# The causal mask of stick-breaking attention, moved from VectorE into the score matmuls

## What is computed

```python
def stick_breaking_attention(q, k, v):
    scale = 1.0 / math.sqrt(q.shape[-1])
    def block(args):
        qb, i = args
        z = jnp.einsum('bhqd,bhkd->bhqk', qb, k) * scale
        q_idx = i * Q_BLOCK + jnp.arange(Q_BLOCK)
        strict = key_idx[None, :] < q_idx[:, None]
        log_one_minus = jnp.where(strict, jax.nn.log_sigmoid(-z), 0.0)
        suffix = lax.cumsum(log_one_minus, axis=3, reverse=True) - log_one_minus
        w = jnp.where(strict, jnp.exp(jax.nn.log_sigmoid(z) + suffix), 0.0)
        return jnp.einsum('bhqk,bhkd->bhqd', w, v)
```

## Time and profile before

| | |
|---|---|
| runs | 2357.04, 2357.75 (median), 2361.81 us |
| profiled execution | 2354.45 us |
| its span, first to last instruction | 2352.7 us |
| mean granted clock of PE, share of full speed | 0.975 |
| PE busy | 2206.1 us, 94% |
| DVE busy | 1676.1 us, 71% |
| ACT busy | 908.8 us, 39% |
| the stick stage | 1963.2 to 2092 us of the span |
| the soft stage | 2092 to 2205 us |

### The profile page before, as it was taken

The page is one execution under the profiler, slowest core; times in us unless marked ns, Lnnn a source line. Parts: engine busy times, 40 slices in busy tenths (PEclk is TensorE's granted clock), DMA queues, the critical chain, the costliest instruction groups (busy, mean ns, idle before and its releaser), DMA issues. The chain is left out here.

```text
span 2352.7 us, 31764 instructions
## 1 busy us (share of the span) xinstructions
PE 2206.1 (94%) x12629; PEld 1967.4 (84%) x12629; DVE 1676.1 (71%) x2797; ACT 908.8 (39%) x1193; POOL 619.2 (26%) x354
## 2 busy tenths in 40 slices
PE   5999989988999998999999899999999898989997
PEld 2888777876799998999999899999999676667775
DVE  6555677873489999889876787778787646566543
ACT  4222234333233333566653233333333433456423
POOL 0000042322347667333334433333331000000000
PEclk8999999999999999999999999999999899999999
DMA  7667410012237777899999999999996222111222
GB/s 259 207 228 235 158 50 1 1 72 72 90 115 248 248 242 241 316 353 338 358 353 374 373 359 352 353 359 350 357 350 238 79 84 66 51 45 55 81 90 72
DMA packets 177524, 486.59 MB, mean 207 GB/s; under 512 B 13632, under 2 KB 80320, under 8 KB 165856
## 3 DMA queue, kind: packets, MB, share of 16 engines
q1 hardware_dynamic: 140512, 350.33, 43.6%
q0 software_dynamic: 36864, 134.23, 14.8%
HBM read 429.98 MB, written 52.43 MB: 205 GB/s over the span
## 5 line engine op out<-in xcount | busy, mean ns | idle before, releaser
L1087 PE MATMUL ps<-h_high,u_high 128*128 128x384 f32 (+1 forms) x1216 | 428.4, 352 | 22.1 <-POOL u_low L1305 12.4
L1089 PE MATMUL ps<-h_high,u_low 128*128 128x384 f32 (+1 forms) x1216 | 420.3, 346 | 0.0
L1088 PE MATMUL ps<-h_low,u_high 128*128 128x384 f32 (+1 forms) x1216 | 420.1, 345 | 0.0
L1087 PE MATMUL ps<-w_high,v_high 128*128 128x384 f32 x1024 | 343.8, 336 | 7.2 <-DVE w_low L1722 7.2
L1089 PE MATMUL ps<-w_high,v_low 128*128 128x384 f32 x1024 | 342.9, 335 | 0.0
L1088 PE MATMUL ps<-w_low,v_high 128*128 128x384 f32 x1024 | 342.9, 335 | 0.0
L1087 PEld LDWEIGHTS ps<-h_high,u_high 128*128 128x128 f32 x1216 | 230.5, 190 | 36.6 <-POOL u_low L1305 14.6
L1455 ACT ACTIVATE v_high<-v_raw 128x2048 fp32r<-128x2048 f32 x64 | 122.6, 1916 | 347.9 <-PE ps L1089 338.5
L1087 PE MATMUL ps<-h_high,w_high 128*128 128x512 f32 x560 | 227.5, 406 | 16.9 <-DVE w_low L346 4.8
L1089 PEld LDWEIGHTS ps<-h_high,u_low 128*128 128x128 f32 x1216 | 230.2, 189 | 8.0
L1088 PEld LDWEIGHTS ps<-h_low,u_high 128*128 128x128 f32 x1216 | 230.9, 190 | 7.0
(11 more groups left out here) (436 smaller groups left out, 4182.9 us busy)
## 6 DMA issues: line engine op xcount, KB each, us to landing
v_raw<-in_peer_v SPq DMA_DIRECT2D x64, 1024.0 KB, 6.7
w_raw<-in_w SPq DMA_DIRECT2D x95, 512.0 KB, 3.5
u_first<-in_uT SPq DMA_DIRECT2D x32, 1024.0 KB, 6.1
u_second<-in_uT SPq DMA_DIRECT2D x32, 1024.0 KB, 6.2
xT<-in_late_w SPq DMA_DIRECT2D x56, 512.0 KB, 4.5
gelu_up<-gelu SPq DMA_DIRECT2D x128, 192.0 KB, 6.8
gates<-gates_sb SPq DMA_DIRECT2D x12, 2048.0 KB, 12.2
weighted<-gelu_up SPq DMA_DIRECT2D x64, 384.0 KB, 6.8
```

Source lines behind the costliest of these rows:

```text
L1087: pe.matmul(out, wh, mh, start=start, stop=False)
L1088: pe.matmul(out, wh, ml, start=False, stop=False)
L1089: return pe.matmul(out, wl, mh, start=False, stop=stop)
```

## The change

The 32 stick masks leave DVE. For a stick item PE follows the score matmul with a second one, identity times `cmask[:, 0]`, that accumulates into the last 128 columns of the same bank; `scored` is counted up by this one. ACT's `exps` of a stick item waits for `scored` and no more for `masked`, which from now on counts soft items alone. DVE's two masks ahead of slot 0 go, and in slots 0 to 14 the masks behind each `finish`; the first mask left is that of item 32, in slot 15. Two waits are new: PE waits once for the causal masks (`made`), and ACT before item 0 for DVE's last scaling of `k.xT` (`rt1_copied` at 2), since `rest[:, 0]` is written by that item's sigmoid.

```diff
--- before.py
+++ after.py
@@ -2068,6 +2068,7 @@
                 kind, h, i = items[2 * p]
                 if p == 0:
                     pe.wait_ge(act_read, read_by(BY_ACT, PROJECTED))
+                    pe.wait_ge(made, 3)
                 if p == HALF:
                     pe.wait_ge(act_read, read_by(BY_ACT, soft_ready))
                     pe.wait_ge(dve_read, read_by(BY_DVE, soft_ready))
@@ -2080,8 +2081,11 @@
                         q, key = sq[a, h // 2], sk[a, h // 2]
                     else:
                         q, key = mq[0:QKD, h + s], mk[0:QKD, h + s]
-                    pe.matmul(ps[:, s, 0:width(2 * p)], q[:, i * P:(i + 1) * P], key[:, 0:width(2 * p)], start=True,
-                              stop=True).then_inc(scored, 1)
+                    W = width(2 * p)
+                    last = pe.matmul(ps[:, s, 0:W], q[:, i * P:(i + 1) * P], key[:, 0:W], start=True, stop=kind == "soft")
+                    if kind == "stick":
+                        last = pe.matmul(ps[:, s, W - P:W], k.ident[:], cmask[:, 0, :], start=False, stop=True)
+                    last.then_inc(scored, 1)
 
             def turn(n):
                 pe.wait_ge(ready, n + 1)
@@ -2190,7 +2194,12 @@
             def exps(n):
                 kind, h, i = items[n]
                 W = width(n)
-                act.wait_ge(masked, n + 1)
+                if n == 0:
+                    act.wait_ge(rt1_copied, 2)
+                if kind == "stick":
+                    act.wait_ge(scored, n + 1)
+                else:
+                    act.wait_ge(masked, n - N // 2 + 1)
                 if n >= 4:
                     act.wait_ge(turned, n - 3)
                 if kind == "stick":
@@ -2342,12 +2351,9 @@
                 W = width(n)
                 dve.wait_ge(scored, n + 1)
                 diag = ps[:, n % 2, W - P:W]
-                if kind == "stick":
-                    dve.tensor_tensor(diag, diag, cmask[:, 0, :], ALU.add).then_inc(masked, 1)
-                else:
-                    link(dve.tensor_tensor(diag, diag, cmask[:, 1, :], ALU.add))
-                    link(dve.tensor_reduce(nmax[:, n:n + 1], ps[:, n % 2, 0:W], AX.X, ALU.max, negate=True))
-                    dve.tensor_scalar(nmax[:, n:n + 1], nmax[:, n:n + 1], QKD ** -0.5, None, ALU.mult).then_inc(masked, 1)
+                link(dve.tensor_tensor(diag, diag, cmask[:, 1, :], ALU.add))
+                link(dve.tensor_reduce(nmax[:, n:n + 1], ps[:, n % 2, 0:W], AX.X, ALU.max, negate=True))
+                dve.tensor_scalar(nmax[:, n:n + 1], nmax[:, n:n + 1], QKD ** -0.5, None, ALU.mult).then_inc(masked, 1)
 
             def finish(n):
                 kind, h, i = items[n]
@@ -2409,7 +2415,10 @@
                 if kind in ("sk", "sv"):
                     t = n + 4 * (kind == "sv")
                     dve.wait_ge(rt1_copied, 1)
-                    dve.scalar_tensor_tensor(k.xT[:, t, :], k.xT[:, t, :], col(k, "norm_f", t, t + 1), rt1, ALU.mult, ALU.mult)
+                    last = dve.scalar_tensor_tensor(k.xT[:, t, :], k.xT[:, t, :], col(k, "norm_f", t, t + 1), rt1, ALU.mult,
+                                                    ALU.mult)
+                    if t == KT - 1:
+                        last.then_inc(rt1_copied, 1)
                 if (kind, n) == ("sq", 1):
                     dve.wait_ge(n_sum, 1)
                     for x, (root, bank, size) in enumerate(((rtq, 4, 3 * P), (rtkv, 5, 2 * P))):
@@ -2428,8 +2437,6 @@
                         dve.wait_ge(t_high, G0 + t + 1)
                         dve.tensor_tensor(glo[:, t, :], M[:, t, :], ghi[:, t, :].bitcast(F32), ALU.subtract).then_inc(t_low, 1)
             dve.wait_ge(made, 3)
-            mask(0)
-            mask(1)
             for p in range(slots):
                 for j in fill[p]:
                     if j in FIRST2:
@@ -2438,7 +2445,7 @@
                 for n in (2 * p, 2 * p + 1):
                     if n < N:
                         finish(n)
-                    if n + 2 < N:
+                    if N // 2 <= n + 2 < N:
                         mask(n + 2)
                 if p >= 2 and (p - 2) % TT == TT - 1:
                     store((p - 2) // TT)
```

## The result

The changed kernel takes 2366.34 us (median of 20 runs, 2361.84 to 2371.18), the kernel before beside it 2361.69 us (median of 20, 2357.04 to 2368.47). The ratio is 1.0018, 95% interval 1.0012 to 1.0024: slower by 4.65 us between the medians (half the interval: 1.4 us), where 0.8 us faster was forecast. The prediction took 4.7 us for the least that can be told apart; with 20 runs on each side the interval leaves out 1. The time of 2366.34 lies above the upper end of the range, 2361.2. The profiled execution took 2367.71 us.

What follows compares the result with a forecast made beforehand. Neither PE nor DVE was taken to pace the whole stick stage; DVE savings and slot 12's relief against dearer PE pairs summed to -1.4 to -0.2 us, middle -0.8, giving 2357.0 us, range 2353.2 to 2361.2.

Steps and rivals of the forecast that it cites:

- the shape of the waits: Stick stage: ScalarE's 44.2 us wait stays at some 30 us or more, put down to DVE's finish or product.
- The round trip of slot 6: Slot 6: finish 11 stands behind a DVE mask waiting for scores 6, and PE waits for it; this goes.
- Later stages shift as a block: Soft items and all that follows: unchanged, moving together by about -0.2 to -1.4 us.
- The relief in slot 12: Last `kv` tile starts 0.9 us early, PE's wait shrinks to some 1.5 us; -2.3 to -3.5 us.
- The gate of DVE in slot 14: `sz` 2: gate waited for DVE's own `low`; now PE is the later one, -0.95 to +0.15 us there.
- the price of a pair: Stick score pairs: lost overlap plus two mask products add 0.44, 0.67, 0.88 and 1.10 us by width, 12.4 us a stage.
- The 0.15 us "more at each mask product": Possible group price per product; over some seven PE-paced slots 2.1 us more, 1.3 us above the start.
- rival (b): PE paces from slot 6 to the end: +6.1 us, 2363.9 us; price at each switch 4.5 us more; chance 0.08.
- ScalarE's wait for the last scaling of xT before item 0 lies under its table load: Before item 0: this new ScalarE wait was claimed to cost nothing.
- A mask is 0.3 us of busy time but only 0.21 us of DVE's time line: DVE: 32 masks free 6.7 us at most, 0.42 us a slot where DVE paces; -2.1 us in slots 0 to 4.
- those waits hang on DVE and ScalarE, which get faster, not slower: Argument against (b): PE's waits in slots 9, 12 and 15 depend on engines the edit speeds up.
- It decides from where PE's idle time [...] is used up: Test for (b): whether additions use up PE's 10.7 us idle after 2016, in slots 9, 12 and 15.

Runs made afterwards that it cites:

- the run with zeros: Kernel before, DVE masks kept, plus an identity-times-zeros product on PE behind each stick score: 2368.24 us, ratio 1.0028.
- the kernel with no product: Changed kernel without its 64 mask matmul instructions, stick items left unmasked, changed waits kept: 2360.44 us, ratio 0.9991.
- that with the early wait: Changed kernel with ScalarE's wait for the last scaling of xT moved ahead of its copies of the values: 2365.4 us, ratio 1.0013.

## Why the prediction was wrong

**Right: the shape of the waits.** ScalarE's wait stayed, "some 30 us or more, now put down to DVE's finish or its product": 36.4 us. The round trip of slot 6 was there and went. Later stages shift as a block. The relief in slot 12 came in its size, -3.29 us where -2.3 to -3.5 was given: PE's idle time before the last `kv` tile shrank from 3.86 to 1.12 us, "some 1.5 us" in the prediction, and its matmul ran in 0.50 us instead of 0.79:

```profile
2076.94 0.50 PE L1087 MATMUL ps<-w_high,g_high 128*128 128x512 f32 x1 [1.12 <-ACT mqkv L2181]
```

That the size fits is in part luck. The prediction has this tile start 0.9 us early because DVE and ScalarE get ahead; it started 105.59 us into the stage for 101.67, 3.9 us late. ScalarE's sigmoids in slot 11 waited 1.03 and 0.39 us for PE's products, so DVE's `low` came at 99.35 for 95.30, its finishes behind it (the one that ScalarE waited for is that of item 23, not 24), and the tile last. PE, at scores 12, was late by more: 5.84 us.

The gate of DVE in slot 14 had no wait for PE before and now waits for PE's tile through ScalarE, as the prediction says of `sz` 2:

```profile
2098.14 0.69 DVE L2309 TENSOR_TENSOR gate_tmp<-ps,gate_tmp 128x512 f32<-128x512 f32 x1 [1.10 <-ACT gate_tmp L2190]
```

**Wrong: the price of a pair.** The step "A mask product uses all 128 rows and stands between the two heads, so I take the stick pairs to become as slow as the soft ones" has the right mechanism and the wrong size. Soft pairs are 96 rows deep next to tiles of 128, and take 1.72 us, twice a single score of 0.86, so their rows hold no price for a change of rows; the stick pairs got two of them more than before. The price did stand in the earlier trace rows: a transpose alone ahead of 64-row scores takes 0.37 us and two take 0.59, so 0.15 is left over for each group, and the prediction took that for a price of the group. A pair now adds: one score that lay beside the other (0.85 us at width 512), two products of 0.22 and two changes of about 0.2, or 0.85 + 0.44 + 0.40 = 1.69 us, measured 1.69 from slot 11 to 12. At 384 it is 0.64 + 0.84 = 1.48, measured 1.49 from slot 10 to 11 and again from 14 to 15; at 256, 0.42 + 0.84 = 1.26, measured 1.33 (slot 9 to 10) and 1.27 (13 to 14). At 128, 0.21 + 0.84 = 1.05; slot 0's pair takes 1.50 us from its first score to the tile, for 0.42 before. The prediction had 1.10, 0.88 and 0.67, and expected score pairs of width 512 at 2.1 us; they take 2.77.

For four slots that is 1.69 + 1.48 + 1.26 + 1.05 = 5.5 us instead of 3.1, and 21.9 us instead of 12.4 for the stage. The 0.15 us "more at each mask product" was in the text, but only as an end of the range and over seven slots; it should have been in the sum, at two changes a pair and at 0.2. On the path this step is worth 1.2 us in slots 10 and 11 (3.18 for 2.0) and, with slot 15, 1.6 us in slots 13 to 15 (2.76 - 0.43 = 2.3 us for 1.1 - 0.4 = 0.7). Slots 5 to 9 went from +0.18 to +2.66, 2.5 us where the prediction goes from -1.7 to -0.6, 1.1 us. Together 4.2 us too little, all of it put down to the pairs here, though slots 5 to 9 hold waits too; slot 12 gave back 0.4 more than its middle.

The Trainium skill, TensorEngine Tiling (Array Packing), section Key Properties, says that a change of tiling mode drains the engine. The traces agree, if a drain is what shows as about 0.2 us more at each border between 64 and 128 rows, in either direction, and ahead of the matmuls of 64 columns (0.41 us for 0.24). The prediction cites it and then leaves it to the upper end of the range and to rival (b).

**Wrong: "ScalarE's wait for the last scaling of xT before item 0 lies under its table load".** It lies ahead of the load. With one wait in front of the first sigmoid, the load starts right behind the copies, at 1963.12 in the kernel before; with two, it starts only after 1.04 us of idle time, when the product has been made. The new wait itself was long met: DVE's last scaling ended at 1966.84 us, the load starts at 1972.34. DVE's first `low` comes 4.11 us after the stage's first score, for 3.02. That slot 1 starts 1.04 us late has another cause, PE's dearer pair in slot 0 (1.50 us for 0.42): in the run with zeros, which has no new wait, slot 1 starts at 5.76 us as well.

**Wrong: "A mask is 0.3 us of busy time but only 0.21 us of DVE's time line".** The row was read rightly and the conclusion not. DVE in slot 0, the product of item 0 before (its scan follows at 1972.72), then product and scan in the changed kernel:

```profile
1972.19 0.29 DVE L2363 TENSOR_TENSOR at_w<-at_w,at_prod 128x128 f32<-128x128 f32 x1
...
1981.47 0.29 DVE L2369 TENSOR_TENSOR at_w<-at_w,at_prod 128x128 f32<-128x128 f32 x1
1981.87 0.42 DVE L2366 TENSOR_TENSOR_SCAN at_prod<-at_rest,zeros 128x127 f32<-128x127 f32 x1
```

From product to scan it is now 0.40 us, where 0.53 us passed before with a mask between them (1972.19 to 1972.72): 0.13 gained. The scan starts 0.11 us after the product's 0.29 us have passed; the mask used to fill that gap, and now it lies open. The distance between two `low` steps of DVE fell by 0.25 to 0.28 us a slot (9.16 to 8.88 in the first), not by 0.42. Over four slots that is 1.03 us won, which just makes up for the 1.09 us by which the first `low` was late: the fifth comes at 44.94 us for 44.88, and slot 5 starts 0.18 us late where the prediction has -1.7. That is 1.9 us.

**The balance.** Forecast -0.8; price of a pair +4.2; slot 12 -0.4; table load and masks +1.9: +4.9 us, measured +4.88. The terms are differences of slot starts in one profile of each kernel, so that they add up says little. What the runs show apart from them is 7.5 us for the products and -2.6 for the DVE side. Rival (b), +6.1 us and with the price of each switch 4.5 more, was the case that came, at a size between it and the forecast: its additions were 14.1 us rather than 8.2 (slots 6 to 15 by the prices above), and most of them still went into waits. What speaks against it in the prediction, "those waits hang on DVE and ScalarE, which get faster, not slower", did not hold: they did not run ahead. DVE's fifth `low` was 0.06 us late, and that in slot 12 was 4.05 us late, because DVE and ScalarE wait for PE in turn. From slot 6 on, only in slots 8, 12 and 15 did the waits shrink by more than PE's additions. "It decides from where PE's idle time [...] is used up" was the right test: 10.7 us of idle time there against additions of 14.1.

## What to carry to other kernels

A matmul that is put between two others is costed by its place: here 0.22 us of its own work, 0.2 us at each border between 64 and 128 rows, and the whole of one neighbour if the two ran side by side before. Such a product is put behind both, which made the stage 4.7 us shorter here, or on the rows that its neighbour uses, 7.5 us shorter, though with only half of the mask added. A second wait in front of an activation can hold back its table load too, and an instruction taken from between two dependent ones is worth only what it kept them apart.

## What the runs showed of the hardware

- Changing between matmuls of 64 and of 128 rows costs about 0.2 us, in both directions: a product takes 0.42 us ahead of a 64-row score and 0.24 ahead of a tile of 128 rows and columns, and 64-row scores take 1.05 us for 512 columns, both heads or one alone, ahead of a 128-row matmul. Ahead of matmuls of 128 rows and 64 columns the product takes 0.41.
- Two heads on rows 0 to 63 and 64 to 127 take as long as one: 1.05 us, with mask products on the same rows 1.29.
- The first sigmoid's table load stood behind its waits in the kernels where it has two (0.62 to 1.35 us of idle time ahead of it in five profiles), and ahead of the wait in the five where it has one. The number of waits in the code is not the whole rule: item 32 has two, and in the kernel before its load starts at 2093.08 us, ahead of the end of its mask at 2093.74. What decides stays open.
- Behind a product of 0.29 us the next scan on DVE started after 0.40.
- In some executions slot 0 runs at 1.2 GHz in part, in others at 2.4: the granted clock of its first 6 us was 1.00 in the kernel before, 0.72 in the kernel with no product and 0.50 in that with the early wait. PE had waited 2.2 us before the first score in each of them (2.16, 2.15 and 2.21). Why it falls in one and not in another stays open. At 0.72 DVE's second `low` came when it does at 1.00 (8.89 us after the first for 8.88), at 0.55 it came 1.4 us later.
